# Deferred layer norms in a two-block transformer kernel: the roots go to the next matmul's output, the means out of weight rows and residual

## The reference

```python
for layer in range(DEPTH_2):
    ...                                   # even: conv and sliding window attention; odd: GLA and MLA
    x = layer_norm(ALPHA * x + y, ln_mix_g[layer], ln_mix_b[layer])
    x = layer_norm(ALPHA * x + swiglu(x, ffn_w_gate[layer], ffn_w_up[layer], ffn_w_down[layer]),
                   ln_ffn_g[layer], ln_ffn_b[layer])

def layer_norm(x, g, b):
    mu = xf.mean(-1, keepdims=True)
    var = jnp.mean(jnp.square(xf - mu), -1, keepdims=True)
    return (xf - mu) * lax.rsqrt(var + LN_EPS) * g + b

def swiglu(x, w_gate, w_up, w_down):
    return (jax.nn.silu(x @ w_gate) * (x @ w_up)) @ w_down
```

## Time and profile before

| | |
|---|---|
| time, median of 3 runs | 1013.54 us (1012.83 to 1014.61) |
| the profiled execution, first to last instruction | 1010.7 us |
| TensorE busy | 944.9 us, 93% |
| VectorE busy | 669.1 us, 66% |
| ScalarE busy | 421.5 us, 42% |
| GpSimd busy | 34.2 us, 3% |
| mean granted TensorE clock | 0.967 |
| DMA | 154.73 MB, mean 153 GB/s |

### The profile page before, as it was taken

How to read it: one execution, slowest core, us unless ns; L and a number is a source line. 1 busy time by engine, 2 the same in 40 slices (tenths; PEclk the granted TensorE clock), 3 DMA queues, 4 the chain that set the end, 5 groups by cost and what they waited for, 6 DMA issues and landing times.

```text
span 1010.7 us, 19135 instructions
## 1 busy us (share of the span) xinstructions
PE 944.9 (93%) x7332; PEld 912.9 (90%) x7332; DVE 669.1 (66%) x1108; ACT 421.5 (42%) x628; POOL 34.2 (3%) x48
## 2 busy tenths in 40 slices
PE   6999799999998999988999999969979799999995
PEld 5987799999998999868999999969869699999994
DVE  5857787777777847778555555686986765555555
ACT  6245534444443644544333333247343343333332
POOL 1000000000000000000000000002401000000000
PEclk9999799999998999997999999979989799999997
DMA  7752155555553655322555555515313155555521
GB/s 284 265 171 92 63 170 197 182 184 176 178 183 105 208 173 164 123 84 90 183 185 186 175 181 184 187 41 173 121 42 124 44 167 184 176 181 185 187 83 42
DMA packets 43989, 154.73 MB, mean 153 GB/s; under 512 B 5072, under 2 KB 5802, under 8 KB 43946
## 3 DMA queue, kind: packets, MB, share of 16 engines
q1 hardware_dynamic: 42192, 151.12, 45.0%
q10 hardware_dynamic: 1449, 1.94, 0.6%
q0 software_dynamic: 304, 1.06, 0.4%
HBM read 153.04 MB, written 1.06 MB: 152 GB/s over the span
## 4 chain that ended last, share of the span: by engine, by line
PE 67%; issue 22%; DVE 7%; ACT 3%; DMA 1%; POOL 1%; SPq 0%; POOLq 0%; ACTq 0%; DVEq 0%
PE ps L349 18%; PE ps L350 17%; PE ps L351 17%; PE ps L366 1%; PE ps L533 1%; PE ps L373 1%; PE ps L367 1%; DVE w_lo L1052 1%; PE ps L649 1%; PE ps L408 1%; PE ps L410 1%; PE ps L409 1%; PE ps L450 1%; PE ps L421 1%; DMA raw<-in_stream 1%
## 5 line engine op out<-in xcount | busy, mean ns | idle before, releaser
L1052 DVE TENSOR_TENSOR w_lo<-raw,w_hi 128x1024 fp32r<-128x1024 f32 x284 | 341.2, 1223 | 191.1 <-ACT w_hi L768 190.4
L349 PE MATMUL ps<-op_hi,w_hi 128*128 128x256 f32 x1336 | 378.5, 283 | 0.0
L350 PE MATMUL ps<-op_lo,w_hi 128*128 128x256 f32 x1336 | 378.1, 283 | 0.0
L351 PE MATMUL ps<-op_hi,w_lo 128*128 128x256 f32 x1336 | 378.1, 283 | 0.0
L768 ACT ACTIVATE w_hi<-raw 128x1024 fp32r<-128x1024 f32 x284 | 288.7, 1051 | 67.5 <-PE ps L351 54.1
L349 PEld LDWEIGHTS ps<-op_hi,w_hi 128*128 128x128 f32 x1336 | 256.5, 192 | 1.0 <-DVE w_lo L1052 0.6
L350 PEld LDWEIGHTS ps<-op_lo,w_hi 128*128 128x128 f32 x1336 | 256.5, 192 | 0.0
L351 PEld LDWEIGHTS ps<-op_hi,w_lo 128*128 128x128 f32 x1336 | 256.5, 192 | 0.0
L349 PE MATMUL ps<-mix_hi,w_hi 128*128 128x256 f32 x748 | 216.4, 289 | 1.6 <-issue 1.4
L350 PE MATMUL ps<-mix_lo,w_hi 128*128 128x256 f32 x748 | 212.8, 284 | 0.0
L351 PE MATMUL ps<-mix_hi,w_lo 128*128 128x256 f32 x748 | 212.6, 284 | 0.0
(11 more groups left out here) (225 smaller groups left out, 817.1 us busy)
## 6 DMA issues: line engine op xcount, KB each, us to landing
raw<-in_stream SPq DMA_DIRECT2D x284, 512.0 KB, 3.4
x<-in_x SPq DMA_DIRECT2D x4, 256.0 KB, 6.2
y<-bias_rows POOLq DMA_DIRECT2D x1, 1024.0 KB, 8.5
result<-x SPq DMA_DIRECT2D x4, 256.0 KB, 2.5
proj<-in_gmask ACTq DMA_DIRECT2D x1, 512.0 KB, 5.4
masks<-in_masks ACTq DMA_DIRECT2D x1, 384.0 KB, 4.6
wpool<-in_wpool ACTq DMA_DIRECT2D x1, 256.0 KB, 3.8
pt<-in_p ACTq DMA_DIRECT2D x1, 256.0 KB, 4.7
```

The costliest lines, as they stand in the source:

```text
L349: pe.matmul(o, wh, xh, start=start, stop=False, **kw)
L350: pe.matmul(o, wh, xl, start=False, stop=False, **kw)
L351: return pe.matmul(o, wl, xh, start=False, stop=stop, **kw)
L1052: dve.tensor_tensor(w_lo[:, s, :], raw[:, s, :], fp(w_hi[:, s, :]), ALU.subtract).then_inc(S["split_done"], 1)
```

## The change

Three things are done to the norms of the second part.

1. The mean goes out ahead of time. The mean of z is ALPHA times the mean of x plus the mean of y. A weight unit whose output is y (`centred`: the out units and the down units of both layers, 60 in all) has the mean of each row over its 1024 output features subtracted when it is split: ScalarE runs over the unit once for the sum, waits, and runs again with it as a bias; VectorE's subtraction takes it as a scalar. So y has mean zero. The residual x has its mean subtracted beforehand by GpSimd (`centre_x`), from a mean that GpSimd, one matmul (`mean_of_x`) and one ScalarE copy make (`sum_x`, `copy_mean`).
2. The root is applied to the next product's output. `op_hi` and `op_lo` are split from gain times z as soon as z is there; the squares, their mean and the root are made while `first_chunks` and two more units run, and VectorE multiplies each gate and up chunk by the root.
3. The shift goes through the product as two extra columns of the operand, 256 and 257 (both the same), so that the product of weights and shift comes out as a column of its own, which is added after the root.

x itself, with root, gain and shift, is rebuilt by GpSimd during the FFN (`normed_x`), and in the odd layer by VectorE and ScalarE, since its q, k and v products (now on `mix_hi`/`mix_lo`) and its residual need it. The odd layer's units are in another order, and its copies from PSUM go from ScalarE to VectorE. All FFNs run one turn less in their loop and write the last turn out.

The core of the diff:

```diff
+def centred(u):
+    for first in (U_EV_OUT, U_OD_OUT):
+        if first <= u < first + 8:
+            return True
+    for first in (U_FFN2, U_FFN3):
+        r = u - first
+        if 4 <= r < 3 * NFF and ((r - 4) % 3 == 0 or r == 3 * NFF - 1):
+            return True
+    return False
...
+        op_hi_wide = sb("op_hi", [P, NCH, SEQ + 2], F32R)
+        op_lo_wide = sb("op_lo", [P, NCH, SEQ + 2], F32R)
+        op_hi, op_lo = op_hi_wide[:, :, 0:SEQ], op_lo_wide[:, :, 0:SEQ]
...
+            def sum_x():
+                chained(pool.tensor_tensor(x_sum[:], x[:, 0:4, :], x[:, 4:8, :], ALU.add))
+                chained(pool.tensor_tensor(x_sum[:, 0:2, :], x_sum[:, 0:2, :], x_sum[:, 2:4, :], ALU.add))
+                pool.tensor_tensor(x_sum[:, 0, :], x_sum[:, 0, :], x_sum[:, 1, :], ALU.add).then_inc(S["x_summed"], 1)
+            def centre_x(n):
+                pool.wait_ge(S["x_mean_copied"], n)
+                for i in range(4):
+                    pool.tensor_tensor(pair(x, i), pair(x, i), over(x_mean_sb, 2), ALU.subtract
+                                       ).then_inc(S["x_centred"], 1)
+            def normed_x(gain, shift, layer, scaled):
+                pool.wait_ge(S["rinv_copied"], scaled)
+                for i in range(4):
+                    own.done(pool.tensor_tensor(pair(sq, i), pair(y, i), over(rinv[:, 0:SEQ], 2), ALU.mult))
+                own.settle()
+                for c in range(NCH):
+                    own.done(pool.tensor_scalar(x[:, c, :], sq[:, c, :], vcol(gain, layer * 8 + c),
+                                                vcol(shift, layer * 8 + c), ALU.mult, ALU.add))
+                own.settle()
+                sum_x()
...
+                first_chunks(bank(4, 0, n), bank(5, 0, n), operand, hi, lo)
+                pe.wait_ge(S[free[0]], free[1])
+                square_mean(0)
+                out_chunk(bank(6, 0, n), hi, lo)
+                spread([(0, 0, SEQ), (1, 0, SEQ + P)])
+                out_chunk(bank(7, 0, n), hi, lo)
+                pe.wait_ge(S["rinv_copied"], scaled)
...
+                if centred(split.n):
+                    own.done(act.activation(w_hi[:, s, :], raw[:, s, :], ACT.Copy, scale=-1.0 / D,
+                                            accum_out=row_mean[:, s:s + 1]))
+                    own.settle()
+                    m = act.activation(w_hi[:, s, :], raw[:, s, :], ACT.Identity, bias=row_mean[:, s:s + 1])
...
             for c in range(12):
                 step()
+                if c == 2:
+                    for i in range(4):
+                        act.wait_ge(S["x_scaled"], i + 1)
+                        for k in (2 * i, 2 * i + 1):
+                            own.done(act.activation(x[:, k, :], sq[:, k, :], ACT.Identity, bias=vcol("ln_ffn_b", k),
+                                                    scale=vcol("ln_ffn_g", k)))
+                    own.settle()
+                    for i in range(4):
+                        act.activation(pair(mix_hi, i), pair(x, i), ACT.Copy).then_inc(S["vop_hi"], 1)
+                if 4 <= c < 8:
+                    act.wait_ge(S["evac"], EV_ODD + c + 1)
+                    act.activation(proj[:, 4 + c, :], proj[:, 4 + c, :], ACT.Silu, bias=shift_col[:, c - 4:c - 3]
+                                   ).then_inc(S["gr_done"], 1)
-                if c == 4:
+                if c == 6:
                     act.wait_ge(S["gate_zb"], 1)
...
+            attention(MLA_H, [0, 0, 0, 0, 1, 7], between={1: gla_leaves, 5: lambda: copy_mean(3)})
+            normed_operand("ln_mix_g", "ln_mix_b", 1)
...
+                dve.wait_ge(S["x_centred"], 4 * k + 4)
                 for b in range(4):
                     acc_complete(b)
+                    dve.scalar_tensor_tensor(pair(y, b), pair(x, b), ALPHA, bank2(b), ALU.mult, ALU.add
+                                             ).then_inc(S["z_ready"], 1)
...
+                        own.done(dve.tensor_tensor(g, chunk(4 + 2 * c, 0), rinv[:, 0:SEQ], ALU.mult))
+                        dve.tensor_copy(shift_col[:, c:c + 1], bank(4 + 2 * c, SEQ, 1)
+                                        ).then_inc(S["conv_done"], 1)
...
+                        chained(dve.tensor_tensor(conv[:, c, :], chunk(5 + 2 * c, 0), rinv[:, 0:SEQ], ALU.mult))
+                        dve.wait_ge(S["gate_act"], j + (j0 + 1))
+                        chained(dve.scalar_tensor_tensor(h_fp[:, c, :], conv[:, c, :], bank(5 + 2 * c, SEQ, 1),
+                                                         gate[:, c, :], ALU.add, ALU.mult))
```

More of the change, by code:

```diff
@@ L329, in _ @@
                     inverse_root(6)
-            for i in range(7, len(STATISTICS)):
-                inverse_root(i)
+            pool.wait_ge(S["vop_lo"], 4)
+            sum_x()
+            inverse_root(7)
+            centre_x(3)
+            inverse_root(8)
+            normed_x("ln_mix_g", "ln_mix_b", 1, 4)
+            centre_x(4)
+            inverse_root(9)
         @block.tensor
@@ L673, in _ @@
             for i in range(4):
[L674 removed]
+                token_unit(512, mix_hi, mix_lo, 2 * i, 2, i == 3)
                 if i == 2:
@@ L871, in feed_forward @@
                 hidden_chunk(1, 3)
-                turns = NFF // 2 - 2
+                turns = NFF // 2 - 3
+                per = sum(centred(split.n + i) for i in range(6))
                 with act.Fori(0, turns) as i:
@@ L1170, in layer_norm, with rest @@
+                def rest(c):
+                    return dve.scalar_tensor_tensor(op_lo[:, c, :], y[:, c, :], vcol(gain, layer * 8 + c),
+                                                    fp(op_hi[:, c, :]), ALU.mult, ALU.subtract)
                 for i in range(4):
[L1171 to L1174 removed]
+                    lo_piece(i, rest)
@@ L1175, in layer_norm @@
+                sum_squares(0)
                 sum_squares(1)
-                dve.wait_ge(S["centred"], ln.n)
-                hand_statistic(7, LN_EPS)
-                for c in range(NCH):
-                    own.done(dve.tensor_scalar(y[:, c, :], y[:, c, :], vcol(gain, layer * 8 + c), None, ALU.mult))
-                own.settle()
-                dve.wait_ge(S["spread_done"], stats.n)
-                r = over(chunk(7, 1), 2)
-                def piece(i):
-                    dve.tensor_tensor(pair(sq, i), pair(y, i), r, ALU.mult).then_inc(S["scaled"], 1)
```

359 lines of the change are left out of this document (203 added, 156 removed).

## The result

The changed kernel takes **994.5 us** (median of 4 runs, 994.26 to 998.31) against 1013.18 us for the one before (4 runs, 1012.53 to 1014.61): a ratio of 0.9823, 95% interval 0.9804 to 0.9843, so 1.8% faster. Forecast were 996.3 us and 986 to 1008. The profiled execution has a span of 992.1 us; before it was 1010.7.

A forecast was written before the change was run, and what follows sets the result against it. TensorE was taken to bound the kernel, with time to win only where it stands. Terms -11.2 -7.7 +1.0 +2.5 -5.6 +1.9 +1.9 gave -17.2 us, from the timed median 1013.54 to 996.3 us; range 986 to 1008.

The forecast's parts named there:

- First norm, -11.2: Mixer norm, layer 0: TensorE starts 0.7 us after its last matmul instead of 14.2; 13.7 won, less GpSimd contention: -11.2 us.
- The 2.1 us for GpSimd's turns at h: First norm: h's last three VectorE operations each wait for up to one GpSimd operation; +2.1 of at most 3.4 us.
- Third norm, -7.7: Mixer norm, layer 1: as the first, but a late mean copy costs 2.5 and the half clock 1.0: -7.7 us.
- Second norm, +1.0: Norm into the odd layer: 13 us won are lost again in the VectorE and ScalarE chain to the token unit: +1.0 us.
- Odd layer after that, +2.5: Decay levels and out units: GpSimd's sum blocks VectorE, 2 within 0 and 4, plus 0.5 for ScalarE splits: +2.5 us.
- The doubled splits: Odd layer's out units: ScalarE's weight splits double for centring, 0.5 us.
- Last norm, -5.6: Norm at the kernel's end: mean, its subtraction and the sum ahead of it go; spread at 998.2 against 1003.81: -5.6 us.
- Means, +1.9: Mean matmuls on the path: four single 128x256 plain fp32 matmuls, two rows of 0.24 each: +1.9 us.
- Two columns, +1.9: Matmuls of 258 columns in 96 units of 24: 0.84 ns more for each of 2304: +1.9 us.
- Rival C: The wide operand's odd pitch of 1032 bytes makes matmuls slower: 1013 to 1290 us; chance 0.08.
- Loops at nothing: FFN loops and sliding window attention: centring's second ScalarE passes and added VectorE work are covered by TensorE, costing nothing.
- Rival B: Contention and queues eat most of the gain, through late h and a longer third norm: 1002 to 1010 us; chance 0.17.

The follow-up runs named there:

- the kernel before with wide tiles: The kernel before with only op_hi and op_lo made 258 columns wide in SBUF, matmuls still reading 256: 1006.08 us, ratio 0.9928.
- the experiment: Changed kernel with GpSimd's rebuilding of x in second and third FFN held until h of the first two hidden chunks is split: 991.83 us.
- four moves: Changed kernel with GpSimd's sum early, the mean's copy early, the third FFN's first two steps with their splits, GpSimd's rebuilding of x later: 979.58 us.

## Why the prediction was right, and where it was not

Right in total, and that by luck: two errors of opposite sign. Against the kernel before with wide tiles (1006.1 us) the change wins 11.6 us, not 17.2; another 7 us came with where the tiles lie, which no term had. By its own steps:

- **First norm, -11.2:** -11.8 measured. The 2.1 us for GpSimd's turns at h were 1.9 by the experiment.
- **Third norm, -7.7:** -4.5 up to the down unit; and the third FFN then takes 180.65 us where the second takes 178.19, 2.2 of it in its first triple (10.94 us against 8.70), at half the clock. The step that failed is the first line, "The same, but the residual's mean is copied by ScalarE behind seven splits". That copy was priced rightly: 2.5 and 1.0 for the clock, where the copy moved early gave 2.4 for the first chunks and 1.45 behind them. But the third FFN is not the same as the second: its first two steps have no split, and so the first down unit's split comes behind h on VectorE. Before the change TensorE did not stand there; now that split is the last thing waited for, 2.25 us more, and the clock's loss comes on top. The sum had nothing for either. GpSimd's lock (1.9) is in both FFNs, and was in the sum.
- **Second norm, +1.0:** 0.0 measured. The chain through ScalarE was read rightly: 4.44 us of standing before chunk 11 for about 5, token unit at 53.3 for 54.3. The first chunks came 1.8 us after the last matmul, not 0.9, since in the odd layer they wait for all four pieces of z (their banks hold it); the chain through ScalarE hides it.
- **Odd layer after that, +2.5:** +5.5 against before, +7.1 against the wide tiles. GpSimd's sum was taken at 2 within bounds of 0 and 4, and was 3.7: the middle of a range was the wrong choice where the blocked engine is the chain. The doubled splits were taken at 0.5 and cost nothing. The one matmul pair for the mean is 0.5. Some 3 us against the wide tiles remain. The granted clock is 0.94, 0.83 and 0.95 in the three stretches above; in the kernel with wide tiles it is 1.00 in the same three. 26.6 x 0.06 and 37.7 x 0.05 are 3.5 us if all that time is matmuls, so the clock is enough to explain the rest. With four moves only the first stretch is below full, and the mixer takes 79.8 us, 2.8 more than with wide tiles: 0.5 for the mean and 26.6 x 0.10 = 2.7 by the same working. No run changed the clock and nothing else, so this is argued, not shown. And not all of the clock's loss is the change's: the kernel before had 0.91 and 0.95 in its own second and third stretch (its second here, then the first two of the kernel with four moves):

```profile
732.40:751.00 18.60, 14.60 (x79) 12.29 (x77) 16.16 (x35) 7.34 (x18) 0.00 (x0) 0.91 0.17 58
...
692.70:719.30 26.60, 26.50 (x127) 21.78 (x128) 23.57 (x38) 11.73 (x18) 12.90 (x16) 0.90 0.34 114
719.30:736.00 16.70, 12.10 (x71) 9.98 (x70) 15.79 (x29) 6.80 (x14) 0.00 (x0) 1.00 0.18 64
```
- **Last norm, -5.6:** -6.6.
- **Means, +1.9:** the second FFN's last two triples take 8.87 and 8.80 us against 8.61, 0.45 for one mean; four make 1.8.
- **Two columns, +1.9:** a triple with 48 wide matmuls takes 8.605 us on the mean, one of the first FFN without them 8.56: 0.94 ns a matmul, 2.2 us in all. Rival C, a penalty for the odd pitch, was wrong in its sign: the tiles behind the wider ones came to lie better.
- **Loops at nothing:** right: TensorE is never idle in them. For ScalarE's second passes the kernel without centring shows it.

Rival B was nearest to the truth of the mechanisms: contention, a queue and the third norm's longer wait took 5 to 6 us more than forecast. With the tiles where they were, the time would be about 1013.2 - 11.6 = 1001.6 us, an estimate: the lower edge of B (1002 to 1010), and still within the stated range.

## What to carry to other kernels

When a stall is taken away, look in the ordered code of each place, not of one for all, at what else the next consumer needs: the same norm in front of two FFNs met two different waits, because one had its splits scheduled two units later. An idle engine's work is free only if it does not share something with the engine on the chain; move it to where that one waits for a third. And before a gain is put down to an edit, look at a stretch that the edit does not touch: here it had become 1% faster, and what came with it was over a third of the gain. The same holds for the clock: a stretch that an experiment does not touch can be 1 us slower in one execution than in another.

## What the hardware showed

- **Distance of tiles.** Back-to-back matmuls of 256 columns take 120.0 ns at the full clock with the tiles packed, 118.9 with two of them 64 bytes longer each, and 118.3 with 64 bytes free behind each of the two. The medians of the two kernels are 7 and 9 us lower, 0.7 and 0.9%, not all of it from the loops. No run here shows why.
- **Who waits, VectorE or GpSimd.** While GpSimd's two-operand products ran (456.20 to 461.62), VectorE's cast and subtraction of SBUF tensors took 1.26 and 1.37 us instead of 0.29 and 0.43; its products of PSUM and one SBUF tensor took their usual 0.41. The up product and h in the same stretch, changed kernel; h reads two SBUF tensors and a PSUM column, and took its usual time here but 0.71 at 470.58:

```profile
456.56 0.41 DVE L1400 TENSOR_TENSOR proj<-ps,rinv 128x256 f32<-128x256 f32 x1
457.29 0.49 DVE L1402 SCALAR_TENSOR_TENSOR proj<-proj,ps 128x256 f32<-128x256 f32 x1 [0.32 <-ACT proj L953]
```

  Beside GpSimd's one-operand form (461.73 to 471.72) it was mostly GpSimd that waited. VectorE's split of two SBUF tensors took its usual 1.27 us at 463.03, where another, beside the products, had taken 2.30 (460.41); GpSimd's operations took 1.60 us beside it and 2.83 beside two splits in a row (466.07), and 0.55 to 0.59 at their shortest. The Trainium skill (SBUF — State Buffer, "SBUF: two separate sides") gives a shared port pair to whichever starts first, a GpSimd operation or a VectorE operation in a two-port mode or with two SBUF inputs (this last only against a GpSimd operation that reads SBUF), and lets the other wait. That one of the two waits, and that products with a PSUM input do not take part, agrees with these rows. That the first to start goes ahead does not always: GpSimd's operation at 468.88 started ahead of VectorE's split at 468.95, and took 1.61 us to the split's usual 1.27. The cast has one SBUF input, and no row tells in which mode it ran.
- **The clock after short stands.** A stand of 2 us before the down unit of the second FFN left the granted clock at 1.00 in six executions, and not in a seventh, where the same code's next triple took 10.21 us instead of 8.70. In the third FFN, where TensorE had also stood 3.7 us ahead of the first chunks, stands of 2.0 and 2.3 us at the same place were both followed by half clock.
